# Scaling of the second tile ahead of the whitening of x, and a weight split moved behind a copy of attention weights

## The reference

```
x = x + gmlp(rms_norm(x));   x = x + swiglu_ffn(x)            # "g", then "f0"
x = x + chunked_relbias_attention(x, ...)                     # "a": 16 heads of 64, softmax(q k + bias) v
x = x + swiglu_ffn(x)                                         # "f1"
x = rms_norm(x, final_norm)                                   # end of the first block: x itself is normalised
x = x + 0.5 * swiglu(rms_norm(x, ffn1_norm), wg, wu, wd)      # "f2"
...                                                           # mixer "m", memory cross attention "c", ffn "f3"
```

## Time and profile before

| | us |
|---|---|
| median of 3 runs | 1172.41 |
| lowest, highest | 1171.55, 1172.63 |
| the profiled execution, whole | 1172.13 |
| its span in the profile | 1170.3 |

### The profile page before, as it was taken

How to read it: one execution, slowest core, us unless ns; L and a number is a source line. 1 busy time by engine, 2 the same in 40 slices (tenths; PEclk the granted TensorE clock), 3 DMA queues, 4 the chain that set the end, 5 groups by cost and what they waited for, 6 DMA issues and landing times.

```text
span 1170.3 us, 15455 instructions
## 1 busy us (share of the span) xinstructions
PE 1160.1 (99%) x6009; PEld 968.7 (83%) x6009; DVE 842.7 (72%) x1438; ACT 598.8 (51%) x797; POOL 59.8 (5%) x109
## 2 busy tenths in 40 slices
PE   8999999999999999999999999999999999999998
PEld 7888888888889988888888888888898787888887
DVE  6666577988857768798886665545568877979874
ACT  7744454544355555454445454434567867545441
POOL 1100010000000000000002400000110001000000
PEclk9999999999999999999999999999999999999999
DMA  7744536555445433655443665455355141565540
GB/s 289 288 155 156 210 113 246 216 216 201 173 167 180 149 140 144 243 224 216 186 176 144 239 230 199 177 199 199 122 204 199 38 144 73 196 236 216 216 144 37
DMA packets 34691, 213.58 MB, mean 182 GB/s; under 512 B 4666, under 2 KB 6842, under 8 KB 10042
## 3 DMA queue, kind: packets, MB, share of 16 engines
q1 hardware_dynamic: 34617, 212.59, 49.0%
HBM read 211.53 MB, written 1.05 MB: 182 GB/s over the span
## 4 chain that ended last, share of the span: by engine, by line
PE 96%; DVE 2%; ACT 1%; DMA 0%; POOL 0%; issue 0%; SPq 0%; DVEq 0%; POOLq 0%
PE ps L325 30%; PE ps L327 29%; PE ps L326 29%; PE ps L331 3%; DVE wlo L1559 1%; PE ps L797 1%; PE ps L848 1%; PE ps L669 1%; PE ps L825 0%; DMA raw<-in_w_v 0%; PE ps L649 0%; DVE tmp L1578 0%; ACT whi L1086 0%; PE ps L772 0%; PE ps L858 0%; DVE a_s L1770 0%
## 5 line engine op out<-in xcount | busy, mean ns | idle before, releaser
L1559 DVE TENSOR_TENSOR wlo<-raw,whi 128x2048 fp32r<-128x2048 f32 (+2 forms) x196 | 432.9, 2233 | 62.6 <-ACT whi L1086 62.5
L1086 ACT ACTIVATE whi<-raw 128x2048 fp32r<-128x2048 f32 (+2 forms) x196 | 363.4, 1869 | 124.6 <-DMA raw<-in_w_gu 69.6
L325 PE MATMUL ps<-whi,xThi 128*128 128x512 f32 (+2 forms) x960 | 373.0, 389 | 1.7 <-DVE wlo L1559 0.9
L327 PE MATMUL ps<-whi,xTlo 128*128 128x512 f32 (+2 forms) x960 | 370.7, 386 | 0.0
L326 PE MATMUL ps<-wlo,xThi 128*128 128x512 f32 (+2 forms) x960 | 370.4, 386 | 0.0
L325 PEld LDWEIGHTS ps<-whi,xThi 128*128 128x128 f32 x960 | 180.3, 188 | 39.8 <-DVE wlo L1559 2.2
L327 PEld LDWEIGHTS ps<-whi,xTlo 128*128 128x128 f32 x960 | 180.3, 188 | 36.6
L326 PEld LDWEIGHTS ps<-wlo,xThi 128*128 128x128 f32 x960 | 180.4, 188 | 35.4
L1691 DVE STREAM_TRANSPOSE f_sil<-f_hid 32x128 f32<-32x128 f32 x480 | 145.3, 303 | 10.0 <-DVE f_hid L1683 0.9
L1201 ACT ACTIVATE f_sil<-ps,stats 128x256 f32<-128x256 f32 x88 | 40.7, 470 | 213.6 <-PE ps L327 212.8
L325 PE MATMUL ps<-whi,f_hThi 128*128 128x512 f32 x352 | 139.9, 397 | 0.0
(11 more groups left out here) (289 smaller groups left out, 1180.8 us busy)
## 6 DMA issues: line engine op xcount, KB each, us to landing
raw<-in_w_gu SPq DMA_DIRECT2D x88, 1024.0 KB, 4.9
raw<-in_w_dn SPq DMA_DIRECT2D x44, 1024.0 KB, 5.4
raw<-in_w_u SPq DMA_DIRECT2D x8, 1024.0 KB, 5.8
raw<-in_w_ao SPq DMA_DIRECT2D x8, 1024.0 KB, 5.1
raw<-in_w_v SPq DMA_DIRECT2D x6, 1024.0 KB, 5.0
raw<-in_w_bv SPq DMA_DIRECT2D x4, 1024.0 KB, 5.1
raw<-in_w_bk SPq DMA_DIRECT2D x4, 1024.0 KB, 4.8
raw<-in_w_bq SPq DMA_DIRECT2D x4, 1024.0 KB, 4.8
```

Of the source, the lines that this page charges most:

```text
L325: e.matmul(ps, a[0], b[0], start=start, stop=False)
L327: return e.matmul(ps, a[1], b[0], start=False, stop=stop)
L1086: e.activation(dst[:, cs], raw_cols(i, cs), ACT.Copy).then_inc(*inc("whi", i, p))
L1559: e.tensor_tensor(lo[:, cs], raw_cols(i, cs), hi[:, cs].bitcast(F32), ALU.subtract).then_inc(*inc("wlo", i, p))
```

## The change

Three edits of order; no instruction is added or removed.

- DVE, entry to f2: `whiten(0)` moves behind the scaling of tile 1 (two `scale`, two `scaled_lo`).
- ACT, entry to f2: the square sum of the whitened x[0] moves behind the high parts of tile 1. The square sum for the final norm stays in front of them. The pair for tile 1 keeps its place behind `gated(0, 0)`.
- DVE, attention: in group 0 the split ahead of `turned_p(0, 0)` moves behind it, ahead of `turned_p(0, 2)`. Groups 1 to 3 keep their order.

```
-        def white(t):
+        def residual_squares(t):
             e.wait_ge(*at("res", "f1", t, 1))
             if t:
                 e.wait_ge(*at("ssq", "f2", 0))
             square_sum("fin", t, x[t][:, :])
+
+        def white_squares(t):
             e.wait_ge(*at("white", t))
             square_sum("f2", t, x[t][:, :])
 
+        def second_squares():
+            residual_squares(1)
+            white_squares(1)
+
         for h in range(2):
             scaled_hi("f2", 0, h)
-        white(0)
+        residual_squares(0)
         for h in range(2):
             scaled_hi("f2", 1, h)
+        white_squares(0)
...
-        ffn("f2", chunks(1, [3, *[3] * 9, 1], beside), lambda: white(1))
+        ffn("f2", chunks(1, [3, *[3] * 9, 1], beside), second_squares)
...
                 residual(before, 1, h, banks[1][h], factor)
+            scaled(S, 1, spare, g)
             if whiten:
                 whiten(0)
-            scaled(S, 1, spare, g)
...
-                if g != 1:
+                if g > 1:
                     split()
                 turned_p(g, 0)
+                if g == 0:
+                    split()
                 turned_p(g, 2)
```

## The result

| | before | after |
|---|---|---|
| median of 16 runs, us | 1172.3 | 1174.36 |
| lowest to highest | 1171.22 to 1172.87 | 1173.77 to 1174.87 |
| span of the profiled execution | 1170.3 | 1172.7 |

The ratio is 1.0019, with a 95% interval of 1.0012 to 1.0025: the change makes the kernel slower, by 2.1 us in the medians and 0.19% in the ratio. The interval lies on the slower side of 1 and holds the 0.2% that I had taken as the limit of what can be told. The span grew by 2.4 us, for which I had 2.35. In the kernel after, the lines behind the first edit are numbered 7 to 9 higher (L1797 for L1790, L2267 for L2258).

What follows compares the result with a forecast made beforehand. PE, busy 99% of the span, was taken as the bound. Attention's -0.46 us and late whiten(0)'s +2.81 took the span from 1170.3 to 1172.65; the median was forecast as 1172.41 - 0.5 + 2.8 = 1174.7, range 1171.2 to 1176.2.

Steps and rivals of the forecast that it cites:

- Attention, 0.46 us: Attention, group 0: with the split behind head 0's copy, PE reaches the product with v 0.46 us earlier.
- The removed wait at gu(0,1), 0.67 us: Entry to f2: PE no longer waits for tile 1's low part and starts gu(0,1) 0.67 us earlier.
- `whiten(0)` 2.81 us later: Entry to f2, DVE: behind two scalings and two low parts, whiten(0) starts at 633.58, 2.81 us later.
- Unit 111: Middle of gu(1,0): its split on DVE moves to 641.3 to 643.6, giving PE a new wait of some 1.1 us.
- turn(1,0): f2, chunk 1, tile 0: PE waits for the later hid and is there 2.15 us later than before.
- turn(2,0): f2, chunk 2, tile 0: no slack against hid, so the whole 2.81 us appears here, replacing the earlier delays.
- turn(0,1): f2, chunk 0, tile 1: PE would wait for hid or its low part; no size given.
- `posz` and SyncE's list as the last link: f2: POOL's late posz delays SP's loads of units 116 to 118, their splits and chunk 2's hid by 2.8 us.
- Nothing comes back: Rival: at f2 the late whiten(0) is hidden by missed slack, the 1.13 us gain stays, 1171.3; chance 0.14.
- faster: Rival, whole kernel: faster by over 0.2%, needing 2.34 us, twice the idle time the change can remove; chance 0.04.
- Part is absorbed: Rival at f2: POOL and SP catch up, only chunk 1's hid path binds, 1.7 us, time 1174.1; chance 0.08.
- One more meeting of POOL and DVE: Third rival, f2: POOL's masks meet one more split, costing 0.7 to 2.28 us, time 1175.4 to 1177.0; chance 0.14.

Runs made afterwards that it cites:

- e1: The kernel before with the attention edit alone: 1171.88 us, ratio 0.9997 (0.9988 to 1.0006) to the kernel before.
- e3: The kernel before with ACT's edit alone, whiten(0) on DVE kept in its early place: 1173.93 us, ratio 1.0015 to the kernel before.
- e2: The kernel before with the two edits at the entry to f2 alone (DVE and ACT): 1174.87 us, ratio 1.0023 to the kernel before.
- e8: The whole change measured once more against the kernel before: 1174.54 us, ratio 1.0022 (1.0013 to 1.003).
- e12: The changed kernel with one split of f2 moved from chunk 0 to chunk 2: 1172.62 us, ratio 1.0005 to the kernel before.
- e4: The changed kernel with POOL's posz memset moved ahead of the factors of f2: 1173.86 us, ratio 1.0015 to the kernel before.

## Why the prediction was right

- *Attention, 0.46 us.* 0.47 in the trace of the change and in that of e1, and 0.47 and 0.44 at the entry to f2. That the later split costs nothing, which the prediction only argued, holds at least up to there. The time of e1 alone doesn't separate the gain from nothing.
- *The removed wait at gu(0,1), 0.67 us.* It went (633.73 follows without a gap), and it was worth nothing, as worked out: PE came earlier to splits and transposes that were later.
- *`whiten(0)` 2.81 us later.* 2.83. e3 shows with another cause (1.7 instead of 2.8, DVE's order untouched) that the lateness of the square sum is what arrives.
- *The steps of the delay.* Unit 111: wait 1.05 (1.1 forecast). turn(1,0): 1.94 later, 2.18 with the offset (2.15 forecast). turn(2,0): 2.79 with the offset (2.81 forecast), which is nearer than it can be relied on, as the same order gave 2.60 and 3.13 in the profiles of e2 and e8. turn(0,1), for which I had expected a wait without giving it a size, is 1.25 later with the offset. That these are not added up but replace one another shows in e12 and e4: without the last ones the earlier ones arrive as late as with them (turn(1,0) in e4, unit 111 and turn(0,1) in e12). The load of unit 118 is issued 0.91 us behind that of unit 116 (656.70, 657.61) and not 0.97; nothing hangs on it, as all of them move together.
- *`posz` and SyncE's list as the last link.* Shown by e4 for its 0.7 us. Without this link the delay is that of turn(1,0) and the low part behind it, some 2.2 (e4's 1.75 and the 0.46 of attention).
- *The sum.* Span +2.35 forecast, +2.4 measured; time +2.3 forecast, +2.1 in 16 runs, +2.6 in the repetition. The profiled execution took 1174.51, forecast 1174.5. The forecast of 1174.7 for the median was 0.3 us high; 0.1 of this is its base, 1172.41 from three runs where sixteen have 1172.3. For the rest I can't say of which term it is: it is no larger than the difference between the two measurements of the same kernel, or than what the last link varies by. The range on record, 1171.2 to 1176.2, is wide enough to take in most of the rivals, so that the time lies within it says little; the steps above carry the account.
- *The rivals.* "Nothing comes back" (1171.3) and "faster" are out. "Part is absorbed" needed POOL to catch up; `posz` kept the full shift. "One more meeting of POOL and DVE" did not lengthen the path in the profile of the change; in that of e8 turn(2,0) came 0.34 us later still, of which 0.18 stand at `posz` already, far below the 0.7 to 2.28 of the rival.

Open: the side of 0.2% on which the change lies. The ratio 1.0019 with its interval of 1.0012 to 1.0025, and 1.0022 in the repetition, can't tell it, and I had put the chances at 0.51 and 0.45.

## What to carry to other kernels

A wait on the path of the bounding engine is worth its length only if no second path lies just behind it: before moving the work that causes it, follow that work's own results to the bounding engine and note the slack at each arrival. Here the wait was 0.67 us, the slack of the other path nothing, and the moved work 2.8 us late. Where several arrivals are late, the largest counts and not the sum, and freeing the last ones (here by giving chunk 0 one split less) was worth 1.7 us in the changed kernel, more than the wait that was visible at first; the same look is needed at the place to which work is moved.

## What I had not expected of the hardware

GpSimd's mask constructions meet DVE's splits, and which instruction is hit can differ from one execution to the other while the end hardly does. GpSimd's timelines of the kernel after, and of the same kernel repeated as e8:

```profile
653.23 0.25 POOL L2222 TENSOR_TENSOR m_every<-ident 128x30 f32<-128x30 f32 x1
653.56 2.68 POOL L2224 TENSOR_TENSOR m_every<-m_every,ident 128x30 f32<-128x30 f32 x2
```

```profile
653.30 2.36 POOL L2222 TENSOR_TENSOR m_every<-ident 128x30 f32<-128x30 f32 x1
655.74 0.58 POOL L2224 TENSOR_TENSOR m_every<-m_every,ident 128x30 f32<-128x30 f32 x2
...
658.39 0.10 POOL L2231 MEMSET m_pos<- 128x1 int32 x1
```

An addition of 30 columns took 0.25 us in the kernel after, where it lay ahead of the split of unit 115 (653.51 to 655.80), and 2.36 in e8, where it began 0.04 behind the start of that split and ended 0.11 behind its end (653.26 to 655.55). In the kernel after the next two additions, begun 0.05 behind the split's start, took 2.68 together, in e8 0.58. Either way `posz` comes at nearly the same time: 28.18 and 28.36 us behind the transposes of tile 1. My third rival had priced such a meeting at up to 2.28 us on top. Here it was not one more meeting but the same one, moved by one instruction, and in these two executions the path over `posz` hangs on the end of DVE's split.
